# Gate matrix stage: the up product spread as one part in every quad of tokens, its last two parts, its GELU and its spill moved a block on

## What is computed

```
    eidx = jnp.take_along_axis(cand_idx, cpos, axis=-1)
    gate = jax.nn.softmax(vals, axis=-1)
...
        act = jax.nn.gelu(jnp.einsum('chkd,cd->chk', u_tab[ec].astype(jnp.float32), xc.astype(jnp.float32)))
        return jnp.einsum('chk,chkd->cd', gc * act, v_tab[ec].astype(jnp.float32))
```

## Time and profile before

| | |
|---|---|
| median of 3 runs | 2358.27 us (2357.53 to 2360.04) |
| the profiled execution | 2357.71 us, its span 2356.0 us |
| gate matrix stage, within the span | about 1089 to 1298 us |
| busy over the span | PE 92%, PEld 80%, DVE 71%, ACT 36%, POOL 31% |
| mean granted clock of PE | 0.949 of full speed |

### The profile page before, as it was taken

The page is one execution under the profiler, slowest core; times in us unless marked ns, Lnnn a source line. Parts: engine busy times, 40 slices in busy tenths (PEclk is TensorE's granted clock), DMA queues, the critical chain, the costliest instruction groups (busy, mean ns, idle before and its releaser), DMA issues. The chain is left out here.

```text
span 2356.0 us, 36614 instructions
## 1 busy us (share of the span) xinstructions
PE 2159.2 (92%) x11561; PEld 1894.3 (80%) x11561; DVE 1667.9 (71%) x3771; ACT 837.3 (36%) x1565; POOL 738.0 (31%) x651
## 2 busy tenths in 40 slices
PE   7986998876799999996999899999999999999989
PEld 5555887543599889996888788998899999999978
DVE  6556122656465368998999677887998989898853
ACT  2130122552332223344887333332332333333331
POOL 0520221203133355552444222223433333333303
PEclk9997799778899999997999899999999999999999
DMA  5206433505223234334666777888887878787711
GB/s 214 26 29 133 147 108 116 178 1 176 100 79 92 87 129 155 132 134 179 195 195 185 289 296 296 307 305 316 297 304 282 305 281 309 278 311 278 271 58 41
DMA packets 194282, 448.24 MB, mean 190 GB/s; under 512 B 26433, under 2 KB 109635, under 8 KB 184643
## 3 DMA queue, kind: packets, MB, share of 16 engines
q1 hardware_dynamic: 137314, 222.02, 28.7%
q0 software_dynamic: 44288, 156.92, 19.6%
q10 hardware_dynamic: 12576, 67.97, 7.3%
HBM read 394.07 MB, written 54.80 MB: 191 GB/s over the span
## 5 line engine op out<-in xcount | busy, mean ns | idle before, releaser
L2788 PE MATMUL e_ps<-w_hi,v_hi 128*128 128x448 f32 x512 | 190.2, 372 | 11.8 <-DVE w_lo L2656 7.1
L2477 ACT ACTIVATE v_hi<-v_raw 128x512 fp32r<-128x512 f32 x256 | 158.6, 624 | 99.1 <-PE e_ps L2800 47.1
L1646 PE MATMUL e_ps<-x_hi,u_hi 128*128 128x448 f32 x512 | 187.9, 367 | 5.5 <-DVE u_lo L2586 5.5
L2800 PE MATMUL e_ps<-w_hi,v_hi 128*128 128x448 f32 x512 | 187.7, 367 | 4.4 <-issue 4.4
L2788 PE MATMUL e_ps<-w_lo,v_hi 128*128 128x448 f32 x512 | 189.1, 369 | 0.0
L2788 PE MATMUL e_ps<-w_hi,v_lo 128*128 128x448 f32 x512 | 189.1, 369 | 0.0
L1646 PE MATMUL e_ps<-x_lo,u_hi 128*128 128x448 f32 x512 | 187.6, 366 | 0.0
L1646 PE MATMUL e_ps<-x_hi,u_lo 128*128 128x448 f32 x512 | 187.6, 366 | 0.0
L2800 PE MATMUL e_ps<-w_hi,v_lo 128*128 128x448 f32 x512 | 187.6, 366 | 0.0
L2800 PE MATMUL e_ps<-w_lo,v_hi 128*128 128x448 f32 x512 | 187.6, 366 | 0.0
L1994 POOL TENSOR_TENSOR r_u_lo<-r_u_raw,r_u_hi 128x1024 fp32r<-128x1024 f32 x50 | 136.3, 2727 | 145.1 <-ACT r_u_hi L1946 145.1
(11 more groups left out here) (577 smaller groups left out, 5655.5 us busy)
## 6 DMA issues: line engine op xcount, KB each, us to landing
v_raw<-in_v_tab ACTq DMA_DIRECT2D x62, 1024.0 KB, 7.5
u_raw<-in_u_tab SPq DMA_DIRECT2D x64, 512.0 KB, 6.2
mixT<-gate_scr SPq DMA_DIRECT2D x32, 896.0 KB, 6.2
gate_scr<-gate_stage SPq DMA_DIRECT2D x13, 2048.0 KB, 9.3
r_u_raw<-in_u_tab SPq DMA_DIRECT2D x50, 512.0 KB, 3.9
gelu_scr<-mixT SPq DMA_DIRECT2D x32, 448.0 KB, 2.7
acts_and_rows<-gelu_scr SPq DMA_DIRECT2D x16, 896.0 KB, 8.1
m_w_raw<-in_w_mix SPq DMA_DIRECT2D x24, 512.0 KB, 3.5
```

The costliest lines, as they stand in the source:

```text
L1646: mm = pe.matmul(out, as_r(u), as_r(x[:, i, 0:TD]), start=(i == 0 and n == 0), stop=(i == KD - 1 and n == 2))
L2477: nc.scalar.activation(as_r(v_hi[:, c % 4]), v_raw[:, c // 4, c % 4], ACT.Copy).then_inc(v_hi_made, 1)
L2788: mm = nc.tensor.matmul(ps[:, c, 0:TD], as_r(v[:, c % 4, e]), as_r(w[b][:, e]), start=(first and e == 0 and n == 0), stop=(last and e == E ...
L2800: mm = nc.tensor.matmul(ps[:, 4 + c % 4, 0:TD], as_r(v[:, c % 4, e]), as_r(w[b][:, e]), start=(e == 0 and n == 0), stop=(e == EG - 1 and n ...
```

## The change

PE does one part after every quad instead of none, two or one: after quads 2 to 7 parts 0 to 5 of the block's own product, and after quads 0 and 1 parts 6 and 7 of the product of the block before. So a product is finished after quad 1 of the next block. ACT does its GELU ahead of quad 7's copy in that next block, and then rounds `u_hi` for the block that comes next (before: for the one after that). SP spills a pair of products ahead of the store of block `b` = 0 of the next pair instead of ahead of that of `b` = 1. The first pair is taken out of the loops of SP, PE and ACT, since in its first block there is no earlier product. Behind the last block PE does the two parts that are left, ACT the last GELU, and SP the last spill. DVE's and POOL's programs stay as they are. The count of products, GELUs, copies, loads and stores stays the same.

```diff
--- before.py
+++ after.py
@@ -2153,7 +2153,8 @@
         assert 2 * UPS == NTB
         QUADS = TB // 4
 
-        PARTS = [0, 2, 2, 1, 1, 1, 1]
+        LATE_PARTS = 2
+        assert QUADS == KD
         block = ctx.enter_context(nc.Block())
 
 
@@ -2165,22 +2166,26 @@
                 sp.dma_start(u_raw[:, b].rearrange("p k n -> p (k n)"),
                              k.d["u_tab"][bass.ds(n + FIRST, 1)].rearrange("o p f -> (o p) f")).then_inc(u_ld[b], 16)
 
-            def blocks(i, ahead):
+            def spill(i):
+
+                sp.wait_ge(gelu_done, 2 * i + 2)
+                sp.dma_start(k.d["gelu_scr"][bass.ds(i + FIRST // 2, 1)].rearrange("o p f -> (o p) f"),
+                             gelu.rearrange("p e t -> p (e t)")).then_inc(k.spilled_late, 16)
+
+            def blocks(i, ahead, before=None):
                 for b in range(2):
                     if ahead:
 
                         sp.wait_ge(u_lo_made, 2 * i + (b + 1))
                         load_u(2 * i + (b + 2), b)
-                    if b == 1:
-
-                        sp.wait_ge(gelu_done, 2 * i + 2)
-                        sp.dma_start(k.d["gelu_scr"][bass.ds(i + FIRST // 2, 1)].rearrange("o p f -> (o p) f"),
-                                     gelu.rearrange("p e t -> p (e t)")).then_inc(k.spilled_late, 16)
+                    if b == 0 and before is not None:
+                        spill(before)
 
                     sp.wait_ge(copied, 2 * QUADS * i + (QUADS * b + QUADS + 4))
                     if b == 1 and not ahead:
                         sp.dma_start(k.d["gate_scr"][0:2, :, NTB - 1, :].rearrange("g p f -> p g f"),
                                      stage[:, 1, 0:2].rearrange("p g t e -> p g (t e)")).then_inc(k.gm_first, 16)
+                        spill(UPS - 1)
                         return
                     sp.dma_start(k.d["gate_scr"][:, :, bass.ds(2 * i + b, 1), :].rearrange("g p o f -> p g (o f)"),
                                  stage[:, b].rearrange("p g t e -> p g (t e)")).then_inc(k.gm_stored[b], 16)
@@ -2198,9 +2203,10 @@
                              k.d["v_tab"][:, 0, 2048 * half:2048 * half + 2048]).then_inc(k.v_ld[half], 16)
             for e in range(EG):
                 sp.dma_start(k.u_raw[:, e].rearrange("p k n -> p (k n)"), k.d["u_tab"][EG * EARLY_GROUPS + e]).then_inc(k.u_ld[e], 16)
-            with sp.Fori(0, UPS - 1) as i:
-                blocks(i, True)
-            blocks(UPS - 1, False)
+            blocks(0, True)
+            with sp.Fori(0, UPS - 2) as i:
+                blocks(i + 1, True, before=i)
+            blocks(UPS - 1, False, before=UPS - 2)
 
         @block.vector
         def _(dve):
@@ -2240,10 +2246,12 @@
 
         @block.tensor
         def _(pe):
-            def blocks(i):
+            def up_part(b, part):
+
+                return dense_part(nc.tensor, k.x_hi, k.x_lo, u_hi[:, b], u_lo[:, b], ps[:, 4 + b, 0:TD], part)
+
+            def blocks(i, first=False):
                 for b in range(2):
-                    out = ps[:, 4 + b, 0:TD]
-                    done = 0
                     for q in range(QUADS):
 
                         pe.wait_ge(copied, 2 * QUADS * i + (QUADS * b + q + 1))
@@ -2256,19 +2264,23 @@
                             mm = nc.tensor.matmul(ps[:, q % 4, KEYS * (n % 4):KEYS * (n % 4) + KEYS], oh1[:, n % 8], oh2[:, n % 8],
                                                   start=True, stop=True)
                         mm.then_inc(multiplied, 1)
-                        if q < QUADS - 1:
-                            if q == 1:
+                        if q >= LATE_PARTS:
+                            if q == LATE_PARTS:
 
                                 pe.wait_ge(u_lo_made, 2 * i + (b + 1))
-                            for part in range(done, done + PARTS[q]):
-                                mm = dense_part(nc.tensor, k.x_hi, k.x_lo, u_hi[:, b], u_lo[:, b], out, part)
-                            done += PARTS[q]
-                            if q == QUADS - 2:
+                            up_part(b, q - LATE_PARTS)
+                        elif not (first and b == 0):
+                            mm = up_part(1 - b, QUADS - LATE_PARTS + q)
+                            if q == LATE_PARTS - 1:
                                 mm.then_inc(up_done, 1)
 
             pe.sem_inc(multiplied, 2)
-            with pe.Fori(0, UPS) as i:
-                blocks(i)
+            blocks(0, first=True)
+            with pe.Fori(0, UPS - 1) as i:
+                blocks(i + 1)
+            for part in range(QUADS - LATE_PARTS, QUADS):
+                mm = up_part(1, part)
+            mm.then_inc(up_done, 1)
 
         @block.scalar
         def _(act):
@@ -2285,7 +2297,15 @@
                 act.wait_ge(multiplied, 2 * QUADS * i + (QUADS * b + q + 1))
                 nc.scalar.activation(oh1[:, n % 8], apart[:, q % 2], ACT.Relu, bias=one, scale=-1.0).then_inc(third_hot, 1)
 
-            def blocks(i, ahead):
+            def gelu_of(b, done, pairs):
+
+                act.wait_ge(up_done, done)
+                if b == 0:
+
+                    act.wait_ge(k.spilled_late, pairs)
+                nc.scalar.activation(gelu[:, b], ps[:, 4 + b, 0:TD], ACT.Gelu_apprx_tanh).then_inc(gelu_done, 1)
+
+            def blocks(i, ahead, first=False):
                 for b in range(2):
 
                     act.wait_ge(k.gm_stored[b], 16 * i + 16)
@@ -2293,14 +2313,12 @@
                     for q in range(QUADS):
                         if q < QUADS - 1:
                             third_one_hot(i, b, q + 1)
-                        if q == QUADS - 1:
-                            act.wait_ge(up_done, 2 * i + (b + 1))
-                            if b == 0:
-
-                                act.wait_ge(k.spilled_late, 16 * i + 16)
-                            nc.scalar.activation(gelu[:, b], ps[:, 4 + b, 0:TD], ACT.Gelu_apprx_tanh).then_inc(gelu_done, 1)
+                        if q == QUADS - 1 and not (first and b == 0):
+                            gelu_of(1 - b, 2 * i + b, 16 * i + 16)
                             if ahead:
-                                u_high(b, i + 1)
+                                u_high(1 - b, i + b)
+                            elif b == 0:
+                                u_high(1, i)
                         act.wait_ge(multiplied, 2 * QUADS * i + (QUADS * b + q + 3))
                         nc.scalar.activation(stage[:, b, :, 4 * q:4 * q + 4, :].rearrange("p g t e -> p t g e"),
                                              ps[:, q % 4, :].rearrange("p (t g e) -> p t g e", t=4, g=NG),
@@ -2314,9 +2332,11 @@
             act.wait_ge(ld, 16)
             for b in range(2):
                 u_high(b, 0)
-            with act.Fori(0, UPS - 1) as i:
-                blocks(i, True)
+            blocks(0, True, first=True)
+            with act.Fori(0, UPS - 2) as i:
+                blocks(i + 1, True)
             blocks(UPS - 1, False)
+            gelu_of(1, 2 * UPS, None)
 
 
 def experts_stage(nc, k):
```

## The result

The changed kernel takes 2335.97 us (median of 10 runs, 2333.70 to 2349.06), the kernel before in the same session 2356.84 (10 runs, 2353.66 to 2360.04): a ratio of 0.9917 with a 95% interval from 0.9901 to 0.9933. The forecast was 2339, the range 2333 to 2351. The profiled execution took 2333.85 us, its span 2332.2. Some executions, of the kernel before too, are about 12 us longer, and in the two profiled ones among them (e3, e8) the excess lies in what follows the stage, 1067.6 and 1066.1 us against 1054.4 here, so medians of a few runs scatter by several us, and what the experiments tell is read from the gate matrix stage itself.

What follows compares the result with a forecast made beforehand. PE and DVE were taken to wait for each other in turn, neither full. Twelve blocks -18.3, first block -2.0 and end +1.0 sum to -19.3 from 2357.7, giving 2338.4, said as 2339 us; range 2333 to 2351.

Steps and rivals of the forecast that it cites:

- The twelve blocks: Gate matrix stage, blocks 1 to 12: 12.95 us each plus 1.2 for one load, 156.6 against 174.89, -18.3.
- hand-overs: DVE's block: 0.1 us added to the summed 12.85 for hand-overs that no row shows apart.
- The table loads: ACT's loop over pairs: one load expected, in block 1, and none later; 14.1 us less on ACT.
- Even parts: PE's parts, one per quad: DVE becomes the bound and never waits for PE to free a one-hot buffer.
- The clock: PE's granted clock: none of its falls taken to remain; each that remains costs about 1 us.
- a clock of 1.00 from block 1 on: Sign on PE that the forecast is right: no stretches at the lower clock level after the first block.
- PE's wait at the subtraction: PE was still to wait for DVE around the subtraction, about 1 us a block, DVE being the bound.
- The first block: Stage start, PE-bound, 17.29 us: one part less, no first load, shorter stand-still; -2.0, between -0.7 and -3.
- The end: Stage end: last GELU in line, +0.54, and last spill ahead of the gate loads, +0.5; together +1.0 us.
- Loads that stay: Rival on ACT's loop: two loads in each of five passes, subtraction waits 1.2 in each; +6, 2345, chance 0.11.
- No clean bound: Rival on DVE: 13.2 us a block, or 0.4 wait for `u_hi` in each; +3 to +5, 2343, chance 0.13.
- code brought in again at the loops: Rival on PE's loop: code fetched again at each of five turns, 4.35 us each; 22 us, 2360, chance 0.04.

Runs made afterwards that it cites:

- e3: Changed kernel with part 3 of every up product left out on PE; 2337.74 us, ratio 0.9900 to the kernel before.
- e8: Kernel before with ACT's first pair ahead of its loop, doubled parts last, and DVE's subtraction ahead of its wait for quad 1's room; 2344.97 us.
- e4: Changed kernel with DVE's subtraction done twice in every block, first into a tensor nothing reads; 2358.93 us, ratio 0.9988 to the kernel before.
- e11: Changed kernel with ACT making the second one-hots of quads 3 and 6, and GpSimd's one-hots left out; 2336.79 us.
- e1: Kernel before with only ACT's first pair taken out of its loop, leaving one table load of twelve; 2349.99 us.
- e2: Changed kernel with an Exp at the head of each ACT loop pass, putting ten table loads back; 2343.95 us.
- e7: Kernel before with ACT's first pair ahead of its loop and parts ordered 0, 1, 1, 1, 1, 2, 2; 2353.77 us.

## Why the prediction was right, point by point

**The twelve blocks** were to take 12 x 12.95 + 1.2 = 156.6 and took 157.29. The step is right in its parts. DVE is the bound (e3, e4). Its subtraction waits 1.07 at the one table load, where 1.2 was taken, and in no later block, because a DVE that is itself the bound comes later, as argued; the room is 0.31. The 0.07 that a block has too much lies in quads 2 to 6, 1.46 to 1.49 each instead of 1.43: where 0.1 was added for hand-overs for want of a row, GpSimd's 0.2 stands, by e11.

**The table loads**, inferred from what the loops are entered with the earlier trace rows, are one, as forecast. What the prediction did not say is how much of the gain they are: 10.3 of 20.8 in the stage by e1, 6.5 by e2. It wrote them into the sum only through the block's new bound. The load's own time also stands by the trace: the GELU begins 1.29 after its load (1113.97 to 1115.26), as in the earlier trace rows. The 2.66 that the Trainium skill gives (ScalarE: Activation LUTs, "What ACT_TABLE_LOAD costs") is not seen in after either.

**Even parts** were named as the reason why DVE would no longer wait for PE. That DVE's wait would go to nothing was right (16.5 to 0.2), the reason only half so. e8 gets there with doubled parts in the block and none in the next; e7, with the same parts, doesn't. Doubled parts make PE late for a while, and what counts is whether DVE comes to a wait for PE in that while. With the doubles early (before, e1) it does, in the middle of the block, as the prediction read from the earlier trace rows. With the doubles late (e7) it does at quad 1, but only the one-hots need that wait; the subtraction merely stands behind it. The change has no doubles, e8 lets DVE subtract while PE catches up. The prediction looked at the parts alone, not at where in DVE's queue the waits stand.

**The clock.** None of the falls of the later blocks remained, as taken; but the sign that was named, a clock of 1.00 from block 1 on, holds in the first profile and not in the second, which has a fall of 1.4 behind the block with the load. That the profiled execution had none is luck of that size. "Shorter and more even" was the reason; e4 supports it, since falls return with stand-stills of 1.42 to 1.64. Yet e1 and e7 stand still 1.10 in every block, as before did, and show none in their last ten. Before, all blocks but the last two had a second stop just behind the first, of 0.22 to 0.50; whether that made the difference was not tried.

**PE's wait at the subtraction** was to be about 1 a block and shows as 0.41 to 0.43. The rest is in quad 1, which takes 1.94 instead of 1.50 at DVE's pace. 0.43 + 0.44, and 0.15 for the last product ahead of the stand-still, which has none to overlap with (its 0.36 instead of a distance of 0.20), make the 1.02 between 12.0 and 13.02: right in the sum, wrong in where it stands.

**The first block** was the mis-sized term: -2.0, within -0.7 to -3, and it measured -3.85 (17.29 to 13.44, 1090.96 to 1104.40). The clock came up after 8.1 us of the stage instead of 11.5; a start-up at the lower level was in no row taken for this term. From the start of quad 1 on, PE had 3.5 us less at the lower level. A fall of 3.41 us made a block of the kernel before 1.6 to 1.8 longer, so by estimate the earlier rise is worth some 1.7 of the 3.85, and about -2.1 is left for what the prediction named. The earlier rise is luck as far as the traces tell: in all of them but the one of before, e1 with PE's program unchanged among them, the clock comes up 7.9 to 10.0 us after the start of the stage. The kernel after, run once more, has it after 9.9 and 0.7 of the gain back in its first block (14.14 against 13.47 by the subtractions).

**The end** was +1.0 and measured +0.55 (16.14 from the last quad 1 to the next stage, before 15.59). The first wait for gates in the next stage, 7.48 in the earlier trace rows, is now 7.83: 0.35, where +0.5 was taken for the spill.

**The rivals.** Loads that stay would have cost 6; e2 gives 6.5 for them. "No clean bound" came nearest of them: 13.02 lies between the forecast's 12.95 and its 13.2, and what held DVE up is GpSimd beside it, as was said for it. Of code brought in again at the loops there is no trace: the blocks are 13.00 to 13.03 across all turns of PE's loop.

Sum: -17.6 - 3.85 + 0.55 = -20.9, and 0.1 back ahead of the first quad 1: the stage's -20.8, against -19.3. The blocks came 0.7 worse than forecast, the first block 1.85 and the end 0.45 better; that these partly cancel is luck. The lower end of the forecast's own range, 2333, is 2334.6 by the terms that are given for it; the measured time lies inside either.

## What to carry to other kernels

Where two engines wait for each other in turn, look in the queue of each for work that stands behind a wait it does not need, and move that work ahead of the wait: together with one pass of ACT ahead of its loop and the parts in another order it did in the steady blocks what the larger change does. A table load inside a loop can be there only because of the set that the loop is entered with; one pass ahead of the loop takes it away. When a stage is down to one full engine, ask what is next before giving it relief: here GpSimd took the relief back, and ACT's chain stood 0.3 us behind.

## What the runs showed of the hardware

- GpSimd slows VectorE, and by how much depends on the instruction: a subtraction of two inputs (128x512, 1.29 us) held one one-hot of DVE for 1.37 instead of 0.33; one-hots, of one input, cost DVE 0.2 to 0.6 a block of eight. With GpSimd's left out and ACT making two more (e11), DVE's quads took 1.41 to 1.42, so ACT showed no such effect.
- Eleven of twelve table loads of 1.28 us went away without a change to any activation (e1). Their price was not 11 x 1.28 = 14.1 but 10.3, about half of it by the three clock falls that went too. Put back into the kernel after, ten of them cost 6.5: the five ahead of a GELU made the subtraction wait 1.04 to 1.07 each, the other five stood beside other work (e2).
- The granted clock fell to its 1.2 GHz level in three blocks in before (PE still for 1.10, and then for another 0.22 to 0.50 in all blocks but the last two) and in four in e4 (1.42 to 1.64 in most); a fall lasted about 3 us and cost 1.3 to 1.8. Behind a single stop of 1.60 it fell in one profile of after and not in the other. With 0.43 (after) and with 1.10 alone (e1, e7) there was none in the last ten blocks.
